# A model step on one core: the last expert's rows joined from on-chip memory, the other rows' loads and the gating matrices moved

## What is computed

```python
# first block, the end
h = rms_norm(x, norm2_g) * (1.0 + scale_f) + shift_f
# each token: 2 of 32 experts, with gates; per expert rows xb = h[tokens of this expert]
a, b = xb @ w_gate[e], xb @ w_up[e]
out = (jax.nn.silu(a) * b) @ w_down[e]           # rows of 1024
y[token] += out * slot_gate
x = x + gate_f * y
x = rms_norm(x, final_g)
# second block, the beginning
u, v = jnp.split(jax.nn.gelu(rms_norm_2(x, a_norm) @ a_w_in), 2, axis=-1)
v = layer_norm_gain(v, v_gain).reshape(B, S // 128, 128, 8, 128)
z = jnp.einsum('gts,bcsgd->bctgd', w_sp * causal, v) + b_sp.T[None, None, :, :, None]
x = x + (u * z.reshape(B, S, 1024)) @ a_w_out
```

## Time and profile before

| | us |
|---|---|
| median of 3 runs | 2122.56 |
| lowest and highest of them | 2118.98, 2124.18 |
| the profiled execution's own time | 2129.58 |
| its span, first to last instruction | 2127.8 |
| PE busy | 1988.1 (93% of the span) |
| PE weight loads busy | 1593.2 (75%) |
| DVE busy | 1189.3 (56%) |
| ACT busy | 967.6 (45%) |
| POOL busy | 187.7 (9%) |
| DMA | 361.88 MB, 170 GB/s over the span |

### The profile page before, as it was taken

How to read it: one execution, slowest core, us unless ns; L and a number is a source line. 1 busy time by engine, 2 the same in 40 slices (tenths; PEclk the granted TensorE clock), 3 DMA queues, 4 the chain that set the end, 5 groups by cost and what they waited for, 6 DMA issues and landing times.

```text
span 2127.8 us, 22854 instructions
## 1 busy us (share of the span) xinstructions
PE 1988.1 (93%) x8918; PEld 1593.2 (75%) x8918; DVE 1189.3 (56%) x1536; ACT 967.6 (45%) x1467; POOL 187.7 (9%) x245
## 2 busy tenths in 40 slices
PE   4999989999999999879999999998899989999997
PEld 3757757777778777748888888886676768888886
DVE  7676588888888888753543333334344334333323
ACT  2433157878778888624233222223445433222221
POOL 3200110122011110020000000001011110000000
PEclk8999899999999999989999999999999999999999
DMA  8454379999999999742322323222111104322310
GB/s 277 138 172 155 109 253 347 351 344 368 355 355 345 349 337 346 279 158 67 115 79 99 99 88 110 71 89 82 41 59 61 59 30 140 110 87 99 99 40 40
DMA packets 195578, 361.88 MB, mean 170 GB/s; under 512 B 13398, under 2 KB 79707, under 8 KB 195468
## 3 DMA queue, kind: packets, MB, share of 16 engines
q1 hardware_dynamic: 179522, 337.67, 46.1%
q10 hardware_dynamic: 5818, 11.98, 1.5%
q0 software_dynamic: 10128, 10.73, 1.5%
HBM read 364.52 MB, written 20.97 MB: 181 GB/s over the span
## 4 chain that ended last, share of the span: by engine, by line
PE 86%; DVE 7%; DMA 3%; ACT 1%; issue 1%; SPq 1%; POOL 0%; ACTq 0%; DVEq 0%; POOLq 0%
PE ps L263 84%; DVE wlo L210 2%; DMA raw<-in_w_in 1%; PE ps L1955 1%; DVE GM L2029 1%; DMA raw<-in_w_expert_down 1%; PE ps L725 1%; SPq L880 1%; DMA raw<-in_w_expert_gate 0%; DVE wlo L214 0%; ACT whi L191 0%; PE ps L2507 0%; DVE hT5l L260 0%; DVE widelo L2775 0%; PE ps L1172 0%
## 5 line engine op out<-in xcount | busy, mean ns | idle before, releaser
L210 DVE TENSOR_TENSOR wlo<-raw,whi 128x1024 fp32r<-128x1024 f32 (+1 forms) x576 | 672.2, 1217 | 326.2 <-ACT whi L191 323.1
L191 ACT ACTIVATE whi<-raw 128x1024 fp32r<-128x1024 f32 (+1 forms) x576 | 572.9, 1047 | 238.3 <-PE ps L263 219.3
L263 PE MATMUL ps<-hT5h,whi 128*128 128x512 f32 x352 | 138.3, 393 | 6.3 <-DVE wlo L210 6.3
L263 PE MATMUL ps<-hT5l,whi 128*128 128x512 f32 x352 | 138.0, 392 | 0.0
L263 PE MATMUL ps<-hT5h,wlo 128*128 128x512 f32 x352 | 137.9, 392 | 0.0
L263 PE MATMUL ps<-hT3h,whi 128*128 128x512 f32 x352 | 137.0, 389 | 0.6 <-DVE hT3l L260 0.6
L263 PE MATMUL ps<-hT3h,wlo 128*128 128x512 f32 x352 | 136.9, 389 | 0.0
L263 PE MATMUL ps<-hT3l,whi 128*128 128x512 f32 x352 | 136.9, 389 | 0.0
L2372 DVE TENSOR_TENSOR tmpT<-tmpT,ps 128x512 f32<-128x512 f32 x44 | 30.1, 684 | 139.6 <-PE ps L263 139.6
L263 PE MATMUL ps<-whi,XT0h 128*128 128x512 f32 x256 | 102.4, 400 | 0.7 <-DVE XT0l L1979 0.7
L263 PE MATMUL ps<-whi,GTh 128*128 128x512 f32 x256 | 100.8, 394 | 1.7 <-DVE GTl L2033 1.7
(11 more groups left out here) (432 smaller groups left out, 4090.0 us busy)
## 6 DMA issues: line engine op xcount, KB each, us to landing
raw<-in_w_expert_gate SPq DMA_DIRECT2D x64, 1024.0 KB, 8.3
raw<-in_w_expert_up SPq DMA_DIRECT2D x64, 1024.0 KB, 8.5
raw<-in_w_expert_down SPq DMA_DIRECT2D x64, 1024.0 KB, 6.5
raw<-in_ffn_w_gu SPq DMA_DIRECT2D x44, 1024.0 KB, 5.1
raw<-in_ffn_w_down SPq DMA_DIRECT2D x20, 1024.0 KB, 5.0
raw<-in_ada_w SPq DMA_DIRECT2D x24, 512.0 KB, 4.6
raw<-in_w_in SPq DMA_DIRECT2D x8, 1024.0 KB
raw<-in_a_w_in SPq DMA_DIRECT2D x8, 1024.0 KB, 8.5
```

The source lines that it names most:

```text
L191: e.activation(hi[:, c], raw[:, c], ACT.Copy).then_inc(self.S("w_hi"), 1)
L210: e.tensor_tensor(lo[:, c], raw[:, c], hi[:, c].bitcast(F32), ALU.subtract).then_inc(self.S("w_lo"), 1)
L263: return e.matmul(o, l, r, start=start, stop=stop, skip_group_check=True)
```

## The change

1. *Last expert from the chip.* Expert 31's rows are no longer spread to `y_d`. Each join bank gets a third product: `HOT` (slots x tokens, the gate where slot and token belong together) times `YB[1]`. `HOT` is made on POOL at expert 12 (`last_rows_pool`) from the gates, which go through DRAM (`gate_d`) and are gathered by an index that DVE makes at expert 4 (`last_rows_vec`).
2. *Zeros.* As `y_d` now lacks those rows and is read whole, ACT writes zeros over all of it early in the program (4 MB from `ZR`, 4096 pieces of 1 KB).
3. *Pairs loaded early.* `Y2` lies in `XN`, a part of `hT2l` and one new tile, apart from what the last expert uses. SP loads it in eight loads of 512 KB, when `y_out0` and `y_out1` say that experts 0 to 30 have landed, behind the first two `gv` tiles; then `FGa`; then the other two `gv` tiles. `more` waits for no spread unless a body runs. The seven idle products go. The squares' unread output goes to `UT`.
4. *Cap.* In the experts, `take_act` and `take_vec` round no further than the second `gv` tile.
5. *Gating matrices.* Their loads are issued by ACT in the join after block 2's squares, masked by POOL after the join, transposed by PE between the two halves of `gv`, copied by ACT after the first half's gelus; their two banks move accordingly.

```diff
@@ experts_pool
+            e.wait_ge(S("gates"), 1)
+            e.dma_start(gate_d.rearrange("(p i) o -> p (i o)", p=P), small[:, 32:40]).then_inc(S("gates_out"), 16)
+            e.wait_ge(S("y_zero"), 16)
             for n in range(NE):
                 if n + 4 < NE:
                     fetch(e, n + 4)
-                spread(e, n)
+                if n < NE - 1:
+                    spread(e, n)
                 if n == 8:
-                    gating_pool(e)
+                    gates_pool(e)
+                if n == 12:
+                    last_rows_pool(e, own)
@@ take_act (take_vec alike)
+        AHEAD = W.index["gv"][2]
-                W.high(e, j + W.depth(j))
+                W.high(e, min(j + W.depth(j), AHEAD))
@@ more
-            e.wait_ge(S("y_out0"), 16 * (NE // 2))
-            e.wait_ge(S("y_out1"), 16 * (NE // 2))
@@ pairs_sync
+            for tb in range(TB):
+                for k in range(2):
+                    r = k * T + tb * P
+                    e.dma_start(Y2[tb][k], y_d[r:r + P, :]).then_inc(landed(tb), 16)
@@ join_pe
-            R.claim(e, "jn", 0)
-            idle_pe(e, R.bank("jn", 0), 7)
-            e.wait_ge(S("weights"), 2 * TB)
+            e.wait_ge(S("weights"), 2 * TB + 1)
             for tb in range(TB):
-                e.wait_ge(S(f"y_in{tb}"), 16)
+                bs = [R.claim(e, "jn", 2 * tb + h) for h in range(2)]
+                e.wait_ge(S(f"y_in{tb}"), 32)
+                for k in range(2):
+                    for h in range(2):
+                        mm(e, bs[h][:, :], DG[:, k, tb, :], Y2[tb][k][:, h * 512:(h + 1) * 512], k == 0, False)
                 for h in range(2):
...
+                    if tb == 0:
+                        e.wait_ge(*R.done(f"ey{NE - 1}", h))
+                    mm(e, bs[h][:, :], HOT[:, tb * P:(tb + 1) * P], YB[1][:, h * 512:(h + 1) * 512], False, True).then_inc(
+                        *R.fill("jn", 2 * tb + h))
@@ join_act
-            for tb in range(TB):
-                e.dma_start(Y2[:, tb, :, :], y_d.rearrange("(k t p) d -> t p k d", k=2, p=P)[tb]).then_inc(S(f"y_in{tb}"), 16)
...
+                if tb == 2:
+                    gating_loads_act(e)
@@ gmlp_pe
+                if h == 0:
+                    gating_pe(e)
@@ sync
+            W.load(e, more_at + 2)
+            e.wait_ge(*R.full(f"x{NE - 1}", 1))
+            e.wait_ge(S("y_out0"), 16 * (NE // 2))
+            e.wait_ge(S("y_out1"), 16 * (NE // 2 - 1))
+            pairs_sync(e, lambda tb: S(f"y_in{tb}"))
+            e.dma_start(FGa[:, :], g["final_g"].partition_broadcast(P)).then_inc(S("fga"), 16)
             W.load(e, more_at + 4)
             more_sync(e)
-            e.wait_ge(S("y_in3"), 16)
             W.load(e, len(W.items))
```

More of the change, by code:

```diff
@@ L383, in program @@
         DG = sb("DG", [P, 2, TB, P])
+        Y2 = [[XN[:, 2 * tb + k, :] for k in range(2)] for tb in range(2)]
+        Y2.append([same(f"Y2{i}", "hT2l", [P, D], skip=4096 * (1 + i))[:, :] for i in range(2)])
+        Y2.append([same("Y22", "hT2l", [P, D], skip=4096 * 3)[:, :], sb("Y23", [P, D])[:, :]])
         pop()
@@ L404, in program @@
         AS = [W.raw[2][:, 0:D], W.raw[2][:, D:2 * D]]
+        DUMP = [UT[:, 2 * i:2 * i + 2, :].rearrange("p a n -> p (a n)") for i in range(4)]
+        HOT = tmpT[0]
+        HOTI = same("HOTI", "tmpT1", [P, T], I32)
+        gate_d = nc.dram_tensor("gate_d", [2 * T, 1], F32, kind="Internal").ap()
         xn_d = nc.dram_tensor("xn_d", [T, D], F32, kind="Internal").ap()
@@ L1271, in first_act @@
             pool_rows(3)
+            e.wait_ge(S("c_vec"), 9)
+            e.dma_start(y_d.rearrange("(p a) (b n) -> p (a b) n", p=P, n=256),
+                        ZR[:, :].unsqueeze(1).broadcast_to([P, 32, 256])).then_inc(S("y_zero"), 16)
             W.high(e, W.index["o"][1] + 1)
@@ L1730, in route_vec @@
             e.wait_ge(*own.now())
-            e.tensor_tensor(small[:, 36:40], small[:, 32:36], sx(7), ALU.mult).then_inc(*own.up())
+            e.tensor_tensor(small[:, 36:40], small[:, 32:36], sx(7), ALU.mult).then_inc(S("gates"), 1)
             v = R.bank("tok")[:, 0:NBLK]
@@ L1850, in spread, with experts_pool @@
                                  in_=YB[z][:, :], in_offset=None, bounds_check=2 * T - 1, oob_is_err=False).then_inc(S(f"y_out{z}"), 16)
-        def experts_pool(e):
+        def experts_pool(e, own):
             e.wait_ge(S("tokens"), 2)
@@ L1859, in experts_pool @@
                     fetch(e, n + 4)
[L1860 removed]
+                if n < NE - 1:
+                    spread(e, n)
                 if n == 8:
[L1862 removed]
+                    gates_pool(e)
+                if n == 12:
+                    last_rows_pool(e, own)
         WSN = [z[:, :].rearrange("p (g s) -> p g s", g=4) for z in tmpT]
         def gating_loads_act(e):
[L1868 removed]
+            e.wait_ge(*R.full("jn", 2 * TB - 1))
             e.dma_start(BSP[:, :, :].rearrange("p g t -> p (g t)"),
@@ L1883, in gating_pool, with last_rows_pool, last_rows_vec @@
                                 pattern=[[0, 4], [-1, P]], channel_multiplier=1).then_inc(S("ws_masked"), 1)
+        def last_rows_pool(e, own):
+            e.wait_ge(S("gates_out"), 16)
+            e.wait_ge(S("gates"), 2)
+            e.indirect_dma_start(out=LASTG[:, 0:1], out_offset=None, in_=gate_d,
+                                 in_offset=bass.IndirectOffsetOnAxis(ap=LASTI[:, 2:3], axis=0),
+                                 bounds_check=2 * T - 1, oob_is_err=False).then_inc(S("gates_in"), 16)
+            e.iota(HOTI[:, :], pattern=[[1, T]], base=0, channel_multiplier=0).then_inc(*own.up())
+            e.tensor_copy(LASTG[:, 1:2], TOK[:, NE - 1:NE]).then_inc(*own.up())
+            e.wait_ge(*own.now())
+            e.tensor_copy(HOT[:, :], HOTI[:, :]).then_inc(*own.up())
+            e.wait_ge(*own.now())
+            e.wait_ge(S("gates_in"), 16)
+            e.tensor_scalar(HOT[:, :], HOT[:, :], LASTG[:, 1:2], LASTG[:, 0:1], ALU.is_equal, ALU.mult).then_inc(S("weights"), 1)
+        def last_rows_vec(e, own):
+            d, row, block = DST[:, NE - 1:NE], LASTI[:, 0:1], LASTI[:, 1:2]
+            e.tensor_scalar(row, d, P - 1, None, ALU.bitwise_and).then_inc(*own.up())
+            e.wait_ge(*own.now())
+            e.tensor_tensor(block, d, row, ALU.subtract).then_inc(*own.up())
+            e.wait_ge(*own.now())
+            e.tensor_copy(LASTG[:, 2:4], LASTI[:, 0:2]).then_inc(*own.up())
+            e.wait_ge(*own.now())
+            e.tensor_scalar(LASTG[:, 2:3], LASTG[:, 2:3], 8.0, None, ALU.mult).then_inc(*own.up())
+            e.tensor_scalar(LASTG[:, 3:4], LASTG[:, 3:4], 1.0 / P, None, ALU.mult).then_inc(*own.up())
+            e.wait_ge(*own.now())
+            e.tensor_tensor(LASTI[:, 2:3], LASTG[:, 2:3], LASTG[:, 3:4], ALU.add).then_inc(S("gates"), 1)
         def gating_pe(e):
@@ L2031, in experts_vec @@
                     turn_vec(e, n + 1)
+                if n == 4:
+                    last_rows_vec(e, own)
                 e.wait_ge(S("gt_hi"), n + 1)
@@ L2074, in body, with pairs_sync @@
                     e.dma_start(dst, w).then_inc(S(f"more_load{t % 2}"), 16)
+                e.wait_ge(S("more_y"), 16 * (n + 1))
+                pairs_sync(e, lambda tb: S("y_again"))
             more(e, body)
+        def pairs_sync(e, landed):
+            for tb in range(TB):
+                for k in range(2):
+                    r = k * T + tb * P
+                    e.dma_start(Y2[tb][k], y_d[r:r + P, :]).then_inc(landed(tb), 16)
         def more_pool(e):
             def body(n):
-                if n > 0:
+                if n == 0:
+                    for tb in range(TB):
+                        e.wait_ge(S(f"y_in{tb}"), 32)
+                else:
+                    e.wait_ge(S("y_again"), 128 * n)
                     e.wait_ge(S("more_turned"), n)
@@ L2947, in _ @@
             first_pool(e, own)
-            experts_pool(e)
+            experts_pool(e, own)
             more_pool(e)
```

58 lines of the change are left out of this document (28 added, 30 removed).

## The result

| | before | after |
|---|---|---|
| median of the runs, us | 2123.37 (2118.98 to 2126.42, 4 runs) | 2109.25 (2105.4 to 2113.19, 4 runs) |
| ratio to before, 95% interval | 1 | 0.9932 [0.9908, 0.9956] |
| profiled execution: time, span, us | 2129.58, 2127.8 | 2105.4, 2103.7 |

The changed kernel is faster by 0.7%. It was run twice more in the experiments' comparisons, with ratios 0.9936 [0.9913, 0.9959] and 0.9916 [0.989, 0.9942].

What follows compares the result with a forecast made beforehand. TensorE, 86% of the chain, was taken as the bound, so time is won where it stands still. Junction -5.9 us and gating transposes +0.9 sum to -5.0: from 2122.56 to 2117.6 us, range 2110 to 2124.

Steps and rivals of the forecast that it cites:

- Kept: the stall of 4.67 us: At the overflow branch after expert 31's last product: the stall stays, so PE starts the join 4.67 us later, at 907.3.
- a slow clock under it: In the join: PE runs at half rate for its first 5.5 us, which adds 2.75 us.
- 24 matmuls, 20.8 us: In the join: with a third product per half block, 48 instructions of 0.434 us take 20.8 us.
- From the join's end to gv's first product: After the join: X's addition at 931.6 instead of 937.50, gain 5.9 us; from there on the chain is the old one.
- Gating matrices on the path: Between gv's two halves: eight transposes, no longer covered, add 0.9 us.
- what is moved out of or into that stage is worth next to nothing: In the experts' 607 us: PE is busy 571.5 us, so moving work or loads out or in changes next to nothing.
- Masks beside DVE: After the join: two POOL masks beside DVE's hT2l add 0 us, up to 3.1 by full blocking.
- Zeros: From about 101 us: writing 4.2 MB of zeros to y_d adds 0 us, bounds 0 and some 5.
- B: Rival at the branch: no stall, the join ends at 923.7, 7.2 us earlier than forecast: 2110.4 us; chance 0.20.
- C: Rival before the experts: zeros not hidden, late loads add 5 us: 2122.6 us, no change; chance 0.12.
- D: Rival at the join: pair loads not early, the join ends 6.2 us later: 2123.8 us, no change; chance 0.08.
- E: Rival at the branch: instruction fetch stands behind the loads, PE starts at 921, 13.7 us after forecast: 2131.3; chance 0.05.

Runs made afterwards that it cites:

- experiment 2: The changed kernel, with TensorE waiting for the end of its own last product before it reads the table and branches: 2111.78 us, ratio 0.994.
- experiment 1: The kernel before, with TensorE's wait for the spreads moved behind the branch, into the first overflow body: 2123.67 us, ratio 0.9989.
- experiment 10: The changed kernel without the code of the overflow blocks on any engine, so no branch before the join: 2106.73 us, ratio 0.9919.
- experiment 3: The kernel before, with the gating matrices' loads, masks, transposes and FGa's load moved out of the experts: 2123.3 us, ratio 0.9989.
- experiment 4: The changed kernel, with the gating matrices' loads, masks and transposes put back into the experts and HOT made at expert 24: 2113.01 us, ratio 0.9948.
- experiment 9: The changed kernel with the gating matrices loaded on SP behind FGa, masked before the join's checks, transposed right behind the join: 2109.92 us, ratio 0.993.
- experiment 6: The changed kernel without the cap on the roundings ahead: 2112.4 us, ratio 0.9949.
- experiment 7: The changed kernel with the zeros written twice, the second time to a tensor nobody reads: 2111.23 us, ratio 0.9947.
- experiment 12: The changed kernel, unaltered, run a third time: 2107.28 us, ratio 0.9916 to the kernel before.
- experiment 5: The changed kernel, unaltered, run once more: 2109.06 us, ratio 0.9936 to the kernel before.
- experiment 8: The changed kernel with the pair loads held until expert 31's last product: 2116.09 us, ratio 0.9959.
- experiment 11: The kernel before without the seven idle products, the wait ahead of the branch kept: 2124.62 us, ratio 1.0001.

## Why the prediction was wrong

The step that failed is "*Kept: the stall of 4.67 us*". The prediction took a fetch behind the branch to be a fixed price of the branch. The reason it gave for the change's side, "only nothing precedes it", is the very reason why the price went. PE's sequencer (the part that reads its instructions) gets to the branch ahead of the last matmuls: the packet moved while they still ran. If it meets no wait, most of the fetch lies under them (packet at 893 to 894, last product until 895.00, join at 896.24). If it must first wait for work that is already the last, the fetch starts when PE has nothing left: 4.67 us in the kernel before, 7.22 in experiment 2. Experiments 1 and 2 move this wait alone, in both directions, and experiment 10 takes the branch away. The Trainium skill's rule, that a taken branch outside the fetched window must fetch its page before execution goes on (Runtime: NRT & Kernel Launch, Instruction fetch mechanics), agrees with the packet in the trace. That the whole of it costs matmul time was my reading, not the rule's, and the trace of before could not tell the two apart, since there a wait stood ahead.

One table ties the runs together. It gives the packet on q8 nearest to the branch (to 0.25 us) and the first product behind the branch:

| | last product ends | packet | first product behind | packet to product | gap |
|---|---|---|---|---|---|
| before | 902.6 | 908.25 | 911.25 | 3.0 | 8.7 |
| experiment 3 | 897.35 | 903.0 | 905.47 | 2.5 | 8.1 |
| experiment 2 | 896.4 | 900.75 | 903.58 | 2.8 | 7.2 |
| experiment 4 | 901.0 | 900.75 | 903.53 | 2.8 | 2.6 |
| experiment 9 | 892.0 | 891.5 | 894.33 | 2.8 | 2.35 |
| experiment 6 | 892.1 | 891.25 | 894.09 | 2.8 | 1.95 |
| experiment 7 | 894.85 | 893.75 | 896.67 | 2.9 | 1.8 |
| experiment 12 | 896.4 | 895.25 | 897.94 | 2.7 | 1.6 |
| changed | 895.0 | 893.5 | 896.24 | 2.7 | 1.2 |
| experiment 5 | 898.9 | 897.0 | 899.81 | 2.8 | 0.95 |
| experiment 1 | 901.7 | 899.0 | 901.77 | 2.8 | 0.04 |

In all eleven the first product comes 2.5 to 3.0 us after the packet, whatever the gap. So the gap that is left is those 2.8 us less the packet's lead over the last product's end; the prediction's 4.67 was 1.7 us up to the packet and 3.0 behind it. In experiment 2 it was 4.4 and 2.8: what grew under the traffic lies ahead of the packet. That the traffic is its cause wasn't tested. Why the lead differs from one execution to the next (0.2 to 2.7 us) stays open. Experiments 8 and 11 aren't in the table, since there PE waited for the landing of the pairs, and neither is experiment 10, which has no such packet. That q8 carries PE's code is inferred, from this table and from experiment 10.

By the steps of the sum:

- **The start of the join**: predicted 4.67 us after the last product, measured 1.24 (0.95 and 1.57 in the other two): 3.4 us more gain.
- **"a slow clock under it"**, +2.75 us: measured 0. The granted clock stayed at 1.00 after a gap of 1.24 us. This term followed from the first, and in experiments 2, 4, 6, 8 and 9, with gaps of 1.95 us or more, it came, but smaller: 5.1 to 5.6 us for the first eight in place of 3.67, so 1.4 to 1.9. Only in experiments 1 and 11 was it 2.9 to 3.0.
- **24 matmuls, 20.8 us**: 20.85 measured. Right.
- **From the join's end to gv's first product**: 8.2 us against 12.6 before; the prediction's 5.9 less 3.1 counted on 2.8 of gain there and 4.4 came (in experiment 12 only 3.2). Part of the old stretch, too, ran at the slow clock, PEclk 0.91 in 925 to 945; that this is the 1.6 us isn't shown.
- These four, 5.9 + 3.4 + 2.75 + 1.6, are 13.7, the junction's measured difference.
- **Gating matrices on the path**, +0.9: 0.87 measured. Right.
- **"what is moved out of or into that stage is worth next to nothing"**: put at 0 and mis-sized; the traces of experiments 3 and 4 show 3 to 5 us. The sentence rested on "the list of its waits there names no weight load". That list names the last link only: PE waits for GM, and GM had waited for ACT's rounding, and that for a load in a full queue. The two long experts (21.6 and 20.3 us) were in the trace of before.
- **The cap**, no cost: in the changed kernel it costs nothing, but it was worth something that the prediction didn't look for (experiment 6: without it PE waits 1.5 us for YB, and the junction is 4 to 6 us longer in all).
- **Masks beside DVE**, 0: measured 0. The masks run at 923.95, 1.24 us for both, beside hT2l, which takes 0.76 us as it did before. But the prediction's "the trace shows less even for wlo" looked at DVE's side alone. Beside the wlo subtractions it was the masks that took long: 3.08 us for the two in the kernel before, 3.06 in experiments 1 and 4. Beside hT2l, and in experiment 9, where DVE was idle under the first of them, they take some 0.64 us each.
- **Zeros**, 0 within 0 to 5: not contradicted (no wait more on PE in 95 to 140; experiment 7: some 2 us for the second writing).
- **Pair loads without a wait**: right; experiment 8 shows that the junction needs them as much as the missing wait (39.3 us without the one, 39.4 without the other).

Of the rivals, B was the one that came, by the mechanism it named ("if PE's sequencer gets to the branch ahead of its last products"). It said 7.2 us below the forecast; the junction gave 7.8 (13.7 less 5.9), and the experts another 3 to 5. Together these would have made some 2105 to 2107 us, so that the median lies within 1.2 us of B's number is in part luck; the runs' own spread is wider than the difference. C, D and E did not come. D's case was made in experiment 8: its join ended 29.6 us after the last product, against 21.8 in experiment 5. That is 7.8 us, where D had 6.2 over a join that the stall delayed already. E looked for the fetch to be held up by the full queue. Experiment 2 may show some of that, 7.22 us against 4.67, but not 23.

## What to carry to other kernels

In these traces the branch was cheap when the engine's sequencer reached it while work was still queued, and cost the whole fetch when a wait for that work stood ahead of it: put waits behind the branch, into the body that needs them. Work that fills an engine while it waits is only cover if it starts on time; started late it is a delay. And before a load in a full stage is called free, follow the wait list two links back, from the engine that waits to the transfer that made the other one late, and look at single periods, not at the stage's mean.

## What the runs showed of the hardware

- The stall at one and the same branch of PE: 0.04 us and 0.95 to 2.6 us when nothing is waited for ahead, 4.67 with a wait in a quiet queue, 7.22 with a wait in a full one (DMA's share 1.04 in 897 to 906), none without the branch. The first product behind the branch started 2.5 to 3.0 us after the instruction packet in each of eleven traces. I had not expected the small remainder to vary between executions of one kernel (0.95, 1.24, 1.57); it follows the packet's lead.
- At the join the granted clock went with the gap. With 1.82 us or less between the last product and the join it stayed at 1.00 (2.4 GHz). With 1.95 us and more it fell to 0.50 (1.2 GHz) under the first products (experiments 2, 4, 6, 8 and 9), which cost 1.4 to 1.9 us each time. These lengths are no rule for other places: in the changed kernel the clock was at 0.50 under the last expert's products after two waits of 1.58 and 1.68 us, and after the wait of 2.24 us for block 3 it stayed at 1.00 in one execution and fell to 0.50 in another (experiment 12).
- Two masks on GpSimd took 3.06 to 3.08 us while VectorE subtracted with both inputs in SBUF, and 1.24 us beside hT2l, where VectorE reads one of its two large inputs from PSUM.
- A stage that the change doesn't touch, the one before the experts, takes 298.8 to 300.0 us in five executions and 303.8 to 305.2 in eight, of the kernel before's kind and of the changed kernel's (302.0 with the zeros twice). Two single profiles can differ by 4 us from that alone.
